# Adaptive-norm products of two trunk layers: each column group sums 256 columns of a row over all k, instead of a part of the sum over 512 columns

## What is computed

```python
mod     = silu(c)     @ ada_w[l] + ada_b[l]        # (6 * 1024): sh1, sc1, gt1, sh2, sc2, gt2
mod_ctx = silu(c_ctx) @ ada_w[l] + ada_b[l]
z_lat = modulate(rmsnorm(x,   pre_mix_g), sh1,  sc1)  @ w_in   # modulate: h * (1 + scale) + shift
z_ctx = modulate(rmsnorm(ctx, pre_mix_g), csh1, csc1) @ w_in
...                                                 # mixer: attention, pooling, RWKV-7; residual with gt1
...                                                 # mixture of experts: sh2, sc2, gt2
```

## Time and profile before

| | us |
|---|---|
| median of 3 runs | 2445.25 (2444.01 to 2449.5) |
| span of the profiled execution, first to last instruction | 2447.6 |
| its time outside the span | not recorded; the span itself lies among the three runs |
| first stage, to the barrier | 232.4 |
| attention, pooling and RWKV of layer 0 start at | 232.4 |
| PE busy in the span | 2056.4 (84%) |
| DVE, ACT, POOL busy | 794.2, 384.9, 432.3 |
| mean granted clock of PE | 0.917 of full |

### The profile page before, as it was taken

One profiled execution on the slowest core, in us unless ns is written; L12 is line 12 of the kernel. 1 busy time (PEld: TensorE's weight loads), 2 busy tenths in 40 slices (PEclk: granted clock), 3 DMA queues, 4 the chain that ended last, 5 costly groups with the idle time before them and its releaser, 6 DMA issues.

```text
span 2447.6 us, 40983 instructions
## 1 busy us (share of the span) xinstructions
PE 2056.4 (84%) x15851; PEld 1162.1 (47%) x15851; DVE 794.2 (32%) x1651; ACT 384.9 (16%) x822; POOL 432.3 (18%) x601
## 2 busy tenths in 40 slices
PE   5998898788889898898996789788668999999992
PEld 1333476664555444444443356466444444444541
DVE  3212176645471111111112734465461111111114
ACT  0111332221201110111110013132101111111110
POOL 0000001111112222222221110111112322223221
PEclk8999898999879999999998899799879999999996
DMA  9676010003049999999996820100238999999983
GB/s 369 230 272 223 3 44 2 3 11 126 35 169 336 377 390 371 391 376 363 371 384 255 303 92 1 44 3 12 117 156 317 399 381 378 383 382 385 372 346 138
DMA packets 150220, 569.61 MB, mean 233 GB/s; under 512 B 26664, under 2 KB 36776, under 8 KB 116177
## 3 DMA queue, kind: packets, MB, share of 16 engines
q1 hardware_dynamic: 125520, 530.03, 56.8%
q0 software_dynamic: 24576, 37.82, 4.5%
HBM read 567.66 MB, written 46.22 MB: 251 GB/s over the span
## 4 chain that ended last, share of the span: by engine, by line
PE 53%; DMA 28%; DVE 9%; ACT 4%; issue 3%; SPq 2%; POOL 1%; POOLq 0%; DVEq 0%; ACTq 0%; PEldq 0%
DMA arena<-in_exp_w_up_dram 24%; PE pb L1358 11%; PE pb L875 7%; PE pb L1377 4%; PE pb L1361 3%; PE pb L854 3%; PE pb L1058 2%; PE pb L1278 2%; PE pb L812 1%; PE pb L909 1%; PE pb L943 1%; PE pb L1133 1%; PE pb L954 1%; PE pb L1011 1%; PE pb L912 1%
## 5 line engine op out<-in xcount | busy, mean ns | idle before, releaser
L1361 PE MATMUL pb<-arena 128*64 128x256 f32 x3072 | 353.8, 381 | 18.2 <-DMA arena<-in_exp_w_up_dram 17.6
L1358 PE MATMUL pb<-arena 128*128 128x512 f32 x512 | 262.2, 669 | 76.8 <-DMA arena<-in_exp_w_up_dram 70.7
L1361 PEld LDWEIGHTS pb<-arena 128*64 128x64 f32 x3072 | 215.5, 134 | 138.7 <-issue 41.3
L2289 DVE TENSOR_TENSOR arena<-arena,pb 128x128 f32<-128x128 f32 (+1 forms) x128 | 41.4, 323 | 668.8 <-ACT arena L1717 652.6
L854 PE MATMUL pb<-arena 128*128 128x128 f32 x1136 | 158.8, 285 | 63.9 <-DVE arena L1758 55.0
L1358 PEld LDWEIGHTS pb<-arena 128*128 128x128 f32 x512 | 106.8, 214 | 211.9 <-issue 210.6
L854 PEld LDWEIGHTS pb<-arena 128*128 128x128 f32 x1136 | 129.8, 144 | 126.5 <-issue 69.8
L875 PE MATMUL pb<-arena 128*128 128x464 f32 (+3 forms) x480 | 185.2, 544 | 3.4 <-ACT arena L1452 3.4
L1377 PE MATMUL pb<-arena 128*64 128x512 f32 x768 | 186.0, 604 | 1.6 <-DVE arena L2295 1.6
L1717 ACT ACTIVATE arena<-pb 128x128 f32<-128x128 f32 (+1 forms) x128 | 39.4, 308 | 931.8 <-PE pb L1361 466.7
L2334 POOL TENSOR_TENSOR arena<-arena 128x8 f32<-128x8 f32 (+1 forms) x42 | 71.5, 1701 | 576.5 <-DVE arena L1749 311.4
(11 more groups left out here) (300 smaller groups left out, 2687.3 us busy)
## 6 DMA issues: line engine op xcount, KB each, us to landing
arena<-in_exp_w_gate_dram SPq DMA_DIRECT2D x128, 1024.0 KB
arena<-in_exp_w_up_dram SPq DMA_DIRECT2D x128, 1024.0 KB
arena<-in_exp_w_down_dram SPq DMA_DIRECT2D x128, 1024.0 KB, 22.0
arena<-in_ada_w_dram SPq DMA_DIRECT2D x40, 1024.0 KB, 7.6
arena<-y_rows SPq DMA_DIRECT2D x36, 512.0 KB, 6.9
arena<-mod_rows SPq DMA_DIRECT2D x17, 512.0 KB, 6.9
arena<-in_ada_w_dram SPq DMA_DIRECT2D x4, 2048.0 KB, 15.0
arena<-in_w_in_dram SPq DMA_DIRECT2D x4, 1920.0 KB, 16.9
```

The source lines that it names most:

```text
L1358: last = mm(pb[:, 2 + j % 2, :], gT[:, j % 2, k, :], ring_gu[:, j, :, k, :], start=(k == 0), stop=(k == KD - 1))
L1361: last = mm(pb[f * FEW:(f + 1) * FEW, 2 + j % 2, 0:FF], gT_few[:, j % 2, k, :], ring_gu[:, j, :, k, f * P:(f + 1) * P], start=(k == 0), st ...
```

## The change

There are now 12 rows of 1024 columns in `ADA` instead of 24 chunks. Column group g takes the 256 columns from 256 g on, for every k, and sums over all 8 slices itself. So a row is 32 products of 256 columns where it was 16 of 512 (and 2 folds of 512). The finished sums lie in partitions 32 g and 32 g + 1; there is no copy by ACT and no fold. `mod_add` works on 128 partitions x 256 columns, of which 8 partitions mean something. The bias and gain rows come in as 4 partitions of 256 columns (`rows_of`), once for each stream, and go out so.

A row's 4 MB comes in four quarters (two slices k each, all 1024 columns) instead of two chunks of two halves; a quarter of row r + 1 is loaded when the same quarter of row r has been used. The first two rows come in halves of 2 MB. PE does half a row (two quarters) where it did a chunk; `ada_after` still places 20 of these in the same 13 steps. PE waits for row r - 2 to be added, before the first half of row r only.

At the start, `token_roots(0)` stands ahead of the first `mod_add`; `mod_add(0)` waits for its own bias rows alone; `spread` and `take_row` go by row and stream (r, s), and `first_norm(0, 0)` needs only the two of stream 0. SP waits for DVE's first clears (`cs_ready`) before it issues the first weights.

```diff
-        ADA = [(0, c) for c in (2, 3, 0, 1, 4, 5, 6, 7, 8, 9, 10, 11)] + [(1, c) for c in (2, 3, 0, 1, 4, 5, 6, 7, 8, 9, 10, 11)]
+        ADA = [(0, j) for j in (1, 0, 2, 3, 4, 5)] + [(1, j) for j in (1, 0, 2, 3, 4, 5)]
...
-            part = lambda m: 4 + min(max(m, 0), STEPS) * (N_ADA - 4) // STEPS
+            part = lambda m: 4 + min(max(m, 0), STEPS) * (2 * N_ADA - 4) // STEPS
...
+        def ada_used(r, q):
+
+            return 4 * (r - 1) + q + 1
...
+        def rows_landed_before(r):
+
+            return 16 * sum(4 if ada_gain(a) else 2 for a in range(r % 2, r + 1, 2))
...
+            def ada_stream(r):
...
+                for q in range(4):
+                    if r > 2:
+                        sp.wait_ge(ada_part, ada_used(r - 1, q))
+                    else:
+                        sp.wait_ge(ada_part, max(q + 1, 2))
+                    sp.dma_start(ada_ring[q // 2][:, q % 2], w[:, 2 * q:2 * q + 2, :]).then_inc(ada_in[q], 16)
...
+                if r >= 4:
+                    mod_store(r - 2)
+                sp.wait_ge(ada_row, r - 1)
+                ada_rows(r)
...
+            sp.wait_ge(cs_ready, 1)
...
-            def ada_products(n, w, halves):
-
-                for k in halves:
-                    g = k % 4
-                    last = mm(pb[32 * g:32 * g + 32, 2 + n % 2, :], cs[:, k, :], w[:, g, :], start=(k < 4), stop=(k >= 4))
+            def ada_products(r, w, ks):
+
+                for k in ks:
+                    for g in range(4):
+                        last = mm(pb[32 * g:32 * g + 32, 2 + r % 2, 0:256], cs[:, k, :], w[:, k - ks[0], g * 256:(g + 1) * 256],
+                                  start=(k == 0), stop=(k == KD - 1))
                 return last
...
-            def ada_fold(n):
-
-                pe.wait_ge(ada_copy, n + 1)
-                mm(pb[0:2, 2 + n % 2, :], c_("fold"), mod_part[:, n % 2, :], start=True, stop=True).then_inc(ada_sum, 1)
...
+            def ada_half(n):
+
+                r = n // 2
+                if n % 2 == 0:
+                    pe.wait_ge(ada_row, r - 1)
+                for q in range(n % 2 * 2, n % 2 * 2 + 2):
+                    pe.wait_ge(ada_in[q], ada_landed(r, q))
+                    ada_products(r, ada_ring[q // 2][:, q % 2], range(2 * q, 2 * q + 2)).then_inc(ada_part, 1)
+
+            def spread(r, s):
+
+                for g in range(4):
+                    last = mm(pb[:, SPREAD_BANK[r][s] + g // 2, g % 2 * 256:(g % 2 + 1) * 256], pick[:, s, g, :], mod_row[:, r, :], start=True, stop=True)
                 last.then_inc(row_spread, 1)
...
                 pe.wait_ge(ada_in[n], 16)
...
+                ada_products(n // 2, first_ada[:, n], range(n % 2 * 4, n % 2 * 4 + 4)).then_inc(ada_part, 1)
+                if n == 2:
+                    pe.wait_ge(ada_row, 1)
+                    for s in range(2):
+                        spread(0, s)
+            pe.wait_ge(ada_row, 2)
+            spread(1, 0)
+            pe.wait_ge(row_taken, 2)
+            spread(1, 1)
...
-            def ada_copied(n):
-                act.wait_ge(ada_part, 2 * n + 2)
-                if n >= 2:
-                    act.wait_ge(ada_sum, n - 1)
-                ac(mod_part[:, n % 2, :], pb[:, 2 + n % 2, :], ACT.Copy).then_inc(ada_copy, 1)
...
+            def mod_add(r):
+
+                dve.wait_ge(ada_rows_in[r % 2], rows_landed_before(r))
+                dve.wait_ge(ada_part, ada_used(r, 3) if r >= 2 else 2 * (r + 1))
+                own, gain, part = mod_row[:, r % 3], gain_row[:, r % 2], pb[:, 2 + r % 2, 0:256]
...
+            token_roots(0)
             mod_add(0)
+            take_row(0, 0)
             mod_add(1)
-            take_row(0)
-            token_roots(0)
-            mod_add(2)
-            take_row(1)
-            mod_add(3)
-            take_row(2)
-            take_row(3)
-            for i in range(2):
-                first_norm(0, i)
+            take_row(0, 1)
+            take_row(1, 0)
+            first_norm(0, 0)
+            take_row(1, 1)
+            first_norm(0, 1)
             token_roots(1)
```

More of the change, by code:

```diff
@@ L202, in trunk_kernel @@
         x_done = sem("x_done")
-        tokens_in = sem("tokens_in")
+        tokens_in = [sem(f"tokens_in{s}") for s in range(2)]
         bc_in = [sem(f"bc_in{s}") for s in range(2)]
@@ L525, in ada_after, with rows_of, ada_landed, ada_gain @@
         def ada_after(n):
[L527 removed]
+            part = lambda m: 4 + min(max(m, 0), STEPS) * (2 * N_ADA - 4) // STEPS
             return range(part(n - 1), part(n))
[L530 to L551, removed]
+        def rows_of(ap, s):
+            return ap[s:P:32]
+        def ada_landed(r, q):
+            return 16 * r
+        def ada_used(r, q):
+            return 4 * (r - 1) + q + 1
+        def ada_gain(r):
+            return {1: "pre_mix_g", 2: "post_mix_g", 4: "pre_ffn_g", 5: "post_ffn_g"}.get(ADA[r][1])
+        def rows_landed_before(r):
+            return 16 * sum(4 if ada_gain(a) else 2 for a in range(r % 2, r + 1, 2))
+        SPREAD_BANK = ((4, 6), (0, 6))
         SCORE_BANK = (0, 1, 6)
@@ L636, in load_w_in, with ada_last @@
+            def ada_last(r):
+                for a in (r - 1, r):
+                    mod_store(a)
+                sp.wait_ge(mod_out, 32 * (r - 1))
             def load_w_in(l, c):
@@ L873, in _ @@
                             pe.wait_ge(z_ready, seen(z_ready))
+                        elif l == 0 and n == 2:
+                            pe.wait_ge(row_taken, 4)
                         for k in range(KD):
@@ L1771, in _ @@
             for s in range(2):
-                step(V.tensor_scalar(pick[:, s * P:(s + 1) * P], c_("ones")[0:2], c_("ident")[0:2, s:s + 1], None, ALU.mult))
+                for g in range(4):
+                    last = V.tensor_scalar(pick[:, s, g, :], c_("ones"), ident[:, 32 * g + s:32 * g + s + 1], None, ALU.mult)
+            step(last)
             V.tensor_copy(ones_bf, c_("ones"))
@@ L1778, in first_norm @@
                 dve.wait_ge(h_ready, sent(h_ready))
-            def mod_add(n):
-                dve.wait_ge(ada_rows_in[n % 2], 16 * sum(2 if ada_gain(a) else 1 for a in range(n % 2, max(n + 1, 4), 2)))
-                dve.wait_ge(ada_sum, n + 1)
-                own, gain, part = mod_row_at(n), ada_gain_at(n), pb[0:2, 2 + n % 2, :]
-                j = ADA[n][1] // 2
-                if ada_gain(n):
+            def mod_add(r):
+                dve.wait_ge(ada_rows_in[r % 2], rows_landed_before(r))
+                dve.wait_ge(ada_part, ada_used(r, 3) if r >= 2 else 2 * (r + 1))
+                own, gain, part = mod_row[:, r % 3], gain_row[:, r % 2], pb[:, 2 + r % 2, 0:256]
+                j = ADA[r][1]
+                if ada_gain(r):
                     step(V.tensor_tensor(own, part, own, ALU.add))
@@ L1848, in _ @@
                     if l == 0 and i >= 2:
-                        for n in range(4, 6) if i == 2 else range(6, N_ADA):
+                        for n in range(2, 3) if i == 2 else range(3, N_ADA):
                             mod_add(n)
```

126 lines of the change are left out of this document (43 added, 83 removed).

## The result

| | before | with the change |
|---|---|---|
| median, us | 2447.38 (2444.01 to 2450.41, 4 runs) | 2409.1 (2406.37 to 2423.13, 4 runs) |
| ratio of the runs | | 0.9856, 95% interval 0.983 to 0.9882 |
| span of the profiled execution | 2447.6 | 2409.2 |
| time of that execution | not recorded | 2411.02 |
| first stage ends | 232.43 | 193.72 |

The forecast was 2408, range 2399 to 2421. The span lost 38.4 us, the first stage 38.71.

The account below looks back on a forecast made before the run. PE was taken as the bound from 64 to 200 us, after a start of PE-DVE waits. Start -9.5, folds -16.2, idle time -9.7, end -2.9, weight loads +1 sum to -37.3: from 2445.25 to 2408 us, range 2399 to 2421.

Parts of the forecast that it names:

- The start: Up to the first tile's turn: new order of DVE and PE work turns it at 43.2 instead of 52.75, -9.5 us.
- the clock as the largest doubt: In the start: PE work after 30.6 at granted clock 0.50 would give back 6.3 us, leaving 3.2 of the gain.
- The folds: Between conditioning and projection steps: 19 folds of 0.84 to 0.85 us leave PE's chain, -16.2 us.
- The idle time: Between some steps: PE no longer waits for DVE's addition of the chunk before, -9.7 us.
- The end: After the last projection product: only ACT's copy and the barrier remain, 0.9 in place of 3.78, -2.9 us.
- The products: Conditioning half rows: 16 products of 256 columns cost the same as 8 of 512, no change.
- The weights: Quarter loads during the steps: a quarter may be late here and there, above all the last and first, +1 us.
- SP's queue: Row loads and stores: as many DMAs as before for the same columns, so the queue is no longer.
- rival 3: Conditioning half rows run two column groups at a time, 3.69 us each: +40, 2447, no change; chance 0.02.
- rival 4: Conditioning column groups run one after the other, 7.4 us a half row: slower, 2526; chance 0.02.
- Issue cost: Conditioning half rows: 16 more instructions add 40 ns each, 13 us over 20, 2421; chance 0.12.
- Loads as the bound: Weight quarters refill only after use, so two-half steps and the start wait: about +10, 2418; chance 0.12.

Follow-up runs that it names:

- the second pair of medians: The unmodified changed kernel timed anew beside the kernel before, in other runs: 2407.7 us, ratio 0.983.
- spreads_early: Changed kernel with row 0's addition ahead of the squares and its two spreads ahead of the third half row's products: first turn 44.65, stage ends 194.62 us.
- spreads_early_warm: spreads_early with five unread products filling PE's idle gap before the fourth half row's products: first turn 41.53, stage ends 193.18 us.
- fold_back: Changed kernel with one fold-sized product behind each of the 20 half rows, without copy or anyone waiting for it: stage ends 207.94 us.
- fourteen_steps: Changed kernel with the 20 half rows over 14 steps instead of 13: stage ends 193.23 us.
- changed_again: The changed kernel itself, timed anew beside the kernel before: 2407.7 us, ratio 0.983; stage ends 195.98 us.
- before_no_coupling: Kernel before with only its folds reordered, so that the addition PE waits for runs beside a chunk: stage ends 223.26 us.
- columns_128: Changed kernel with each 256-column conditioning product as two of 128, sums not kept right: stage ends 198.38 us.
- group_by_group: Changed kernel with the same products ordered one column group after the other: stage ends 198.14 us.
- before_three_repairs: Kernel before with reordered folds, separate semaphores for the third and fourth chunks' bias rows, and last fold ahead of the last projection step: stage ends 220.56 us.
- first_norm_sooner: Changed kernel with one spread between third and fourth half rows, second stream's spreads and takes later, 14 steps, stores before attention's weights: 2404.52 us, ratio 0.9812.

## Why the prediction was right, step by step

The mechanism held term by term: -37.3 us predicted, -38.7 in the stage. That the medians came within 1.1 us of 2408 is luck in part, since the part behind the stage scatters by 12 us and the second pair of medians differed by 43.6.

- **The start**, -9.5 predicted, -10.06 at the turn. Each event came within 1.2 us: squares from 21.09 (21.7), first addition done 26.44 (26.9), third half row 26.24 (27.4), row 1 added by 35.98 (36.7), turn 42.69 (43.2). Two errors cancelled in part: the third half row was at the lower clock (3.64, not 3.21), and the weights landed earlier than a pitch of 5.67 had them. I named the clock as the largest doubt; spreads_early and spreads_early_warm show that it is: 6 us of doubt had been worked out, and one idle gap of 4.3 us cost the turn 3.1.
- **The projection's first steps**: a term that I didn't have. Turn to projection went 0.7 us faster and the first two steps 1.2 us slower (15.28 for 14.11), net +0.5. The steps were slower because the granted clock stood at 0.50 up to 50 us, 5 us past their start, where before it rose between 58 and 59 us, 3 us past it. Why it rose later isn't shown: in fold_back and fourteen_steps, with the same program up to there, the two steps took 14.27 and 14.22, in changed_again 15.39, so the 1.2 us may not be the change's.
- **The folds**, -16.2. fold_back gives 0.82 us each with its other differences taken off, against 0.84 to 0.85 from the earlier trace rows.
- **The idle time**, -9.7. Gone in the profile; before_no_coupling gives 9.2, net of 1.7 more of waiting for weights.
- **The end**, -2.9 predicted, -3.1 measured.
- **The products**, 0 predicted. 37.8 us for 38.9. Steps with two half rows gain 0.1 us more, because the two run into each other without a fold or an idle stretch between. That the earlier trace rows foretold this shape held, and columns_128 shows the same one halving further.
- **The weights**, +1 predicted, +0.8 (1.8 us of idle time for 1.0). The place was right, two steps of two half rows at the end.
- **SP's queue**: "no longer" was wrong in size. A row or store DMA of 4 partitions took SP 0.50 to 0.53 us in the timeline, one of 2 partitions 0.25 to 0.27. It is as many DMAs and twice the time. The chain passes through four of them at the start, from 2.96 to 5.64 us, ahead of a load that took 19.40; DMA moved 410 GB/s from 10 to 27.5 us, so I take them to cost nothing there, which no run tested. No later wait in the chain comes from them.
- **The rivals.** Two sums in them are slightly off and change nothing: rival 3 comes to 2448, and rival 4 decides from 3.75 / 32 = 0.117 us. Issue cost, group by group and two groups at a time fell by columns_128, group_by_group and the chain's 1.86. Loads as the bound is the one that lies closest behind: every version that started sooner, or took the idle time away, met it (3.8 us in before_three_repairs, 2.3 in first_norm_sooner).

Not settled: why the part behind the stage, identical in program, scatters by 12 us between executions; no run was made for it.

## What to carry to other kernels

Where a sum is split over column groups only to fill the array, give each group other output columns and the whole sum instead: the streamed columns are the same, and the copy, the folding product and the wait between them go. Price a removed product at PE's time in the stream and the wait that it fed apart, since the second can often be had by order alone (12 of 39 us here). And before moving work out of PE's way to an earlier gap, look at the granted clock behind the gap that opens: an idle stretch just ahead of a critical product made it twice as long.

## What the runs showed that I had not expected

- Products of one column group may stand four in a row in the list and still overlap with those of the others (1.97 us for 1.93); with eight in a row they overlap only in part (4.59 for 1.93).
- Products of 128 columns at four groups side by side went at 30 ns a recorded instruction, shorter than the 40 ns of the earlier trace rows.
- Five useless products in an idle gap made the first tile ready 3.1 us sooner than the same kernel without them, 1.2 us sooner than the changed kernel.
- Stores put ahead of the attention's weights let the stage end sooner and the attention wait for its weights: 4.94 us from the barrier to its first product, for 3.75.
- A small DMA costs its issuer more with 4 partitions than with 2, 0.50 for 0.26 us, at the same 4 KB or less.
